# A transformer step on one core: 52 squared down tiles, and the first seven up tiles taken in two token halves

## The reference, cut to what matters

```python
def peer_ffn(h, w_query, sub_keys1, sub_keys2, expert_down, expert_up):
    ...
    expert_idx = jnp.take_along_axis(cand_idx, pos, axis=-1)
    gates = jax.nn.softmax(top_v, axis=-1).astype(h.dtype)
    ...
        u = jnp.take(expert_down, idx_blk, axis=0)
        act = jax.nn.gelu(jnp.einsum('bpd,bphkd->bphk', h_blk, u))
        vv = jnp.take(expert_up, idx_blk, axis=0)
        return jnp.einsum('bphk,bphkd->bpd', g_blk * act, vv)
```

## Time and profile before

| what | us |
|---|---|
| three runs | 1527.0 (1525.01 to 1530.42) |
| profiled execution, its own time | 1524.74 |
| its span | 1523.1 |
| TensorE busy in it | 1483.8 (97%) |
| VectorE, ScalarE, GpSimd busy | 1100.7, 661.1, 426.1 |

### The profile page before, as it was taken

How to read it: one execution, slowest core, us unless ns; L and a number is a source line. 1 busy time by engine, 2 the same in 40 slices (tenths; PEclk the granted TensorE clock), 3 DMA queues, 4 the chain that set the end, 5 groups by cost and what they waited for, 6 DMA issues and landing times.

```text
span 1523.1 us, 25244 instructions
## 1 busy us (share of the span) xinstructions
PE 1483.8 (97%) x9787; PEld 1253.5 (82%) x9787; DVE 1100.7 (72%) x1942; ACT 661.1 (43%) x1013; POOL 426.1 (28%) x285
## 2 busy tenths in 40 slices
PE   8999999999999978999999999999999999999998
PEld 5777878875655577599999999999999888888887
DVE  5888788674675664767888887777776767777776
ACT  4556453643421511334443444444444445455453
POOL 0000000000000200018888888888883000000000
PEclk9999999999999999999999999999999999999999
DMA  9777573357555930456767667777775777777776
GB/s 340 280 247 247 198 261 129 138 206 230 186 207 194 367 133 17 142 167 154 160 146 140 139 145 162 167 161 160 158 162 123 239 237 240 240 241 240 238 239 229
DMA packets 183306, 297.24 MB, mean 195 GB/s; under 512 B 51818, under 2 KB 92546, under 8 KB 183188
## 3 DMA queue, kind: packets, MB, share of 16 engines
q1 hardware_dynamic: 136528, 277.08, 54.8%
q0 software_dynamic: 39296, 8.55, 8.3%
q10 hardware_dynamic: 7364, 9.99, 2.0%
HBM read 276.54 MB, written 19.03 MB: 194 GB/s over the span
## 4 chain that ended last, share of the span: by engine, by line
PE 58%; POOL 26%; issue 7%; DVE 5%; ACT 2%; DMA 1%; ACTq 1%; SPq 0%; DVEq 0%; POOLq 0%
POOL c_dram L2635 26%; PE bank L568 14%; PE bank L570 14%; PE bank L572 14%; PE bank L563 5%; ACTq L2087 1%; PE bank L540 1%; PE bank L918 1%; PE bank L930 1%; PE bank L620 1%; PE bank L929 1%; DVE gt L1291 1%; PE bank L1111 0%; PE bank L613 0%; PE bank L553 0%
## 5 line engine op out<-in xcount | busy, mean ns | idle before, releaser
L2635 POOL DMA_INDIRECT c_dram<-gates,places x256 | 403.6, 1577 | 149.0 <-issue 77.7
L568 PE MATMUL bank<-hT_high,dT_high 128*128 128x256 f32 x1024 | 294.9, 288 | 0.0
L570 PE MATMUL bank<-hT_low,dT_high 128*128 128x256 f32 x1024 | 288.5, 282 | 0.0
L572 PE MATMUL bank<-hT_high,dT_low 128*128 128x256 f32 x1024 | 288.3, 282 | 0.0
L1310 DVE TENSOR_TENSOR dT_low<-bank,dT_high 128x512 fp32r<-128x512 f32 x256 | 164.0, 681 | 91.3 <-ACT dT_high L2528 90.1
L2540 ACT CAST up_high<-slot 128x1024 fp32r<-128x1024 f32 x128 | 134.3, 1049 | 160.9 <-DMA slot<-in_expert_up_dram 160.9
L568 PE MATMUL bank<-up_high,A_high 128*128 128x512 f32 x512 | 199.9, 391 | 1.3 <-DVE A_low L1310 1.3
L570 PE MATMUL bank<-up_low,A_high 128*128 128x512 f32 x512 | 200.7, 392 | 0.0
L572 PE MATMUL bank<-up_high,A_low 128*128 128x512 f32 x512 | 199.2, 389 | 0.0
L568 PEld LDWEIGHTS bank<-hT_high,dT_high 128*128 128x128 f32 x1024 | 194.1, 190 | 0.2 <-issue 0.2
L572 PEld LDWEIGHTS bank<-hT_high,dT_low 128*128 128x128 f32 x1024 | 193.5, 189 | 0.0
(11 more groups left out here) (451 smaller groups left out, 2459.2 us busy)
## 6 DMA issues: line engine op xcount, KB each, us to landing
slot<-in_expert_up_dram SPq DMA_DIRECT2D x128, 512.0 KB, 3.5
slot<-in_expert_down_dram SPq DMA_DIRECT2D x89, 512.0 KB
slot<-in_w_in_dram SPq DMA_DIRECT2D x41, 1024.0 KB, 5.2
slot<-in_expert_down_dram SPq DMA_DIRECT2D x156, 128.0 KB
P<-in_w_ada_dram SPq DMA_DIRECT2D x16, 1024.0 KB, 7.7
c_dram<-zeros SPq DMA_DIRECT2D x1, 16384.0 KB, 50.9
slot<-c_dram SPq DMA_DIRECT2D x128, 128.0 KB, 3.5
slot<-in_w_in_dram SPq DMA_DIRECT2D x6, 2048.0 KB, 8.9
```

What stands on the lines that cost most here:

```text
L568: pe.matmul(o, lhsT=lhs_high.bitcast(F32R), rhs=rhs_high.bitcast(F32R), start=start, stop=False, skip_group_check=True)
L570: pe.matmul(o, lhsT=lhs_high.bitcast(F32R), rhs=rhs.bitcast(F32R), start=False, stop=False, skip_group_check=True)
L572: return pe.matmul(o, lhsT=lhs.bitcast(F32R), rhs=rhs_high.bitcast(F32R), start=False, stop=stop, skip_group_check=True)
L2635: g.indirect_dma_start(C_dram, bass.IndirectOffsetOnAxis(ap=places[:, x, k:k + 1], axis=0), gates[:, x, k:k + 1], None, compute_op=ALU.add ...
```

## The change

`SQUARED` takes two of three tiles above 49 instead of one of two: 52 instead of 39. The ring of up tiles has seven places (`RING`); the three new ones lie where the down tiles were, and are loaded when the last down tiles have been transposed. The up stage is now a list of 135 passes: tiles 0 to 6 for the first 128 tokens, the same tiles for the other 128 tokens, then tiles 7 to 127 whole. A pass of one token half has two banks, 6 matmuls, and operations of 128 columns where there were 256. All counts (`gated`, `weighed`, `tile_done`, the ring of gates) go by the pass number u. The gates of the first passes wait for the scatters of t = 0 alone, those of pass 7 for t = 1. In SyncE's queue the gates of pass p + 4 now stand behind up tile p, which waits until pass p is finished.

```diff
@@ -173,7 +173,8 @@
-    down_in, up_in = [sem(f"down{j}_in") for j in range(3)], [sem(f"up{j}_in") for j in range(4)]
+    RING = 7
+    down_in, up_in = [sem(f"down{j}_in") for j in range(3)], [sem(f"up{j}_in") for j in range(RING)]
...
-    up_tile = [slot[1][:, j * D:(j + 1) * D] for j in range(4)]
+    up_tile = [slot[1][:, j * D:(j + 1) * D] for j in range(4)] + [down_tile[j] for j in (2, 0, 1)]
+    up_low = [carve_at(f"up_low{j}", slot_at + 4 * at * D, D) for j, at in enumerate((4, 5, 6, 7, 2, 0, 1)[0:RING])]
...
+    up_hi_free = [N_KEYS - 3, N_KEYS - 3, N_KEYS - 2, N_KEYS - 2, N_KEYS - 1, N_KEYS - 1, N_KEYS - 1]
+    up_tile_free = {4: N_KEYS - 3, 5: N_KEYS - 2, 6: N_KEYS - 1}
+    FIRST, SECOND, BOTH = range(1), range(1, TT), range(TT)
+    passes = ([(p, FIRST) for p in range(RING)] + [(p, SECOND) for p in range(RING)] +
+              [(p, BOTH) for p in range(RING, N_KEYS)])
+    pass_of = {p: u for u, (p, ts) in enumerate(passes)}
+
+    def up_tokens(u):
+        ts = passes[u][1]
+        return slice(ts.start * P, ts.stop * P)
...
-    SQUARED = [n for n in range(N_KEYS) if n > 49 and n % 2 == 1]
+    SQUARED = [n for n in range(N_KEYS) if n > 49 and n % 3 != 0]
...
+    def pe_tile_up(u):
+        p, ts = passes[u]
+        pe.wait_ge(weighed, u + 1)
         pe.wait_ge(up_split, p + 1)
-        for b in range(4):
-            m = pe_up_part(p, b)
+        for b in range(2 * ts.start, 2 * ts.stop):
+            m = pe_up_part(u, b)
         m.then_inc(tile_done, 1)
...
+    def v_gate(u):
+        p, tok = passes[u][0], up_tokens(u)
         clear(v, ("down", p))
-        v.wait_ge(coeff_in[p % 4], 16 * (p // 4 + 1))
-        v.tensor_tensor(G[:, p, :], G[:, p, :], coeff[p % 4], ALU.mult).then_inc(gated, 1)
+        v.wait_ge(coeff_in[u % 4], 16 * (u // 4 + 1))
+        v.tensor_tensor(G[:, p, tok], G[:, p, tok], coeff[u % 4][:, tok], ALU.mult).then_inc(gated, 1)
...
     def v_experts():
         v_gate(0)
         v_gate(1)
-        v_split_up(0)
-        v_weigh(0)
-        for p in range(N_KEYS):
-            if p + 2 < N_KEYS:
-                v_gate(p + 2)
-            if p + 1 < N_KEYS:
-                v_split_up(p + 1)
-                v_weigh(p + 1)
+        for u, (p, ts) in enumerate(passes):
+            if ts != SECOND:
+                v_split_up(p)
+            v_weigh(u)
+            if u == RING - 1:
+                v_gate(RING)
+                v_gate(RING + 1)
+            elif u != RING - 2 and u + 2 < len(passes):
+                v_gate(u + 2)
...
     def a_split_up(p):
-        a.wait_ge(up_in[p % 4], 16 * (p // 4 + 1))
-        if p > 3:
-            a.wait_ge(tile_done, p - 3)
+        a.wait_ge(up_in[p % RING], 16 * (p // RING + 1))
+        if p < RING:
+            held(a, ("down", up_hi_free[p]))
         else:
-            held(a, ("down", N_KEYS - 3 + p // 2))
-        a.copy(up_hi[p % 4].bitcast(F32R), up_tile[p % 4]).then_inc(up_high, 1)
-
-    def a_weigh(p):
-        a.wait_ge(gated, p + 1)
-        if p > 3:
-            a.wait_ge(tile_done, p - 3)
-        a.copy(A_high[p % 4].bitcast(F32R), G[:, p, :]).then_inc(a_high_made, 1)
+            a.wait_ge(tile_done, pass_of[p - RING] + 1)
+        a.copy(up_hi[p % RING].bitcast(F32R), up_tile[p % RING]).then_inc(up_high, 1)
+
+    def a_weigh(u):
+        p, tok = passes[u][0], up_tokens(u)
+        a.wait_ge(gated, u + 1)
+        if u > 3:
+            a.wait_ge(tile_done, u - 3)
+        a.copy(A_high[u % 4][:, tok].bitcast(F32R), G[:, p, tok]).then_inc(a_high_made, 1)
...
+            if n == N_KEYS - 2:
+                for p in (0, 1):
+                    a_split_up(p)
+                    a_weigh(p)
             if n == N_KEYS - 1:
-                a_split_up(0)
-                a_weigh(0)
+                a_split_up(2)
+                a_split_up(3)
+                a_weigh(2)
             a_tile_gelu(n)
             if n == 1:
                 a_gates(0, range(1, 2), range(1, 2))
             if n in (15, 30, 45):
                 a_gates(n // 15)
-        for p in range(1, N_KEYS):
-            a_weigh(p)
-            a_split_up(p)
+        for u in range(3, RING):
+            a_weigh(u)
+            if u + 1 < RING:
+                a_split_up(u + 1)
+        for u in range(RING, len(passes)):
+            a_weigh(u)
+            if u >= RING + 4 and passes[u - 4][0] + RING < N_KEYS:
+                a_split_up(passes[u - 4][0] + RING)
...
     def s_up(p):
-        if p > 3:
-            sp.wait_ge(tile_done, p - 3)
-        sp.dma_start(up_tile[p % 4], I["expert_up_2"][0][p * P:(p + 1) * P, :]).then_inc(up_in[p % 4], 16)
-
-    def s_coeff(p):
-        if p > 3:
-            sp.wait_ge(gated, p - 3)
-        sp.dma_start(coeff[p % 4], C_dram[p * P * S:(p + 1) * P * S].rearrange("(e n) o -> e (n o)", n=S)
-                     ).then_inc(coeff_in[p % 4], 16)
+        if p >= RING:
+            sp.wait_ge(tile_done, pass_of[p - RING] + 1)
+        elif p in up_tile_free:
+            held(sp, ("turn", up_tile_free[p], 1))
+        sp.dma_start(up_tile[p % RING], I["expert_up_2"][0][p * P:(p + 1) * P, :]).then_inc(up_in[p % RING], 16)
+
+    def s_coeff(u):
+        p, ts = passes[u]
+        if u in (0, RING):
+            for h in range(2):
+                sp.wait_ge(scattered[ts.start][h], 16 * TOPK * PEER_H // 2)
+        if u > 3:
+            sp.wait_ge(gated, u - 3)
+        sp.dma_start(coeff[u % 4][:, up_tokens(u)],
+                     C_dram[p * P * S:(p + 1) * P * S].rearrange("(e n) o -> e (n o)", n=S)[:, up_tokens(u)]
+                     ).then_inc(coeff_in[u % 4], 16)
 
...
         for n in range(3, N_KEYS):
             s_down(n)
-        for t in range(TT):
-            sp.wait_ge(scattered[t][1], 16 * TOPK * PEER_H // 2)
-        for p in range(4):
-            s_coeff(p)
-        for p in range(4, N_KEYS):
-            s_coeff(p)
+        for u in range(4):
+            s_coeff(u)
+        for u in range(4, RING):
+            s_up(u)
+            s_coeff(u)
+        for u in range(RING, RING + 4):
+            s_coeff(u)
+        for p in range(RING, N_KEYS):
             s_up(p)
+            if pass_of[p] + 4 - RING < len(passes):
+                s_coeff(pass_of[p] + 4 - RING)
+        for u in range(len(passes) + 4 - RING, len(passes)):
+            s_coeff(u)
```

More of the change, by code:

```diff
@@ L454, in program @@
     coeff = [slot[0][:, 3 * D + j * S:3 * D + (j + 1) * S] for j in range(4)]
-    up_tile = [slot[1][:, j * D:(j + 1) * D] for j in range(4)]
-    cursor[0] = slot_at + 4 * KT * CW
-    up_low = [carve(f"up_low{j}", D) for j in range(4)]
+    up_tile = [slot[1][:, j * D:(j + 1) * D] for j in range(4)] + [down_tile[j] for j in (2, 0, 1)]
+    up_low = [carve_at(f"up_low{j}", slot_at + 4 * at * D, D) for j, at in enumerate((4, 5, 6, 7, 2, 0, 1)[0:RING])]
     cursor[0] = hT_at
@@ L460, in program @@
     cursor[0] = lasting_top
-    dT_low, dT_high, up_hi = [], [], [None] * 4
+    dT_low, dT_high, up_hi = [], [], []
     for j in range(3):
@@ L472, in program @@
     A_low = [carve(f"A_low{n}", S) for n in range(N_KEYS)]
-    for j, at in enumerate((4 * 4 * D, 5 * 4 * D, 0, 4 * D)):
-        cursor[0] = lasting_top + at
-        up_hi[j] = carve(f"up_high{j}", D)
+    for j, at in enumerate([lasting_top + 4 * x * D for x in (4, 5, 0, 1, 2, 3)][0:min(RING, 6)] + [hT_at][0:RING - 6]):
+        up_hi.append(carve_at(f"up_high{j}", at, D))
+    up_hi_free = [N_KEYS - 3, N_KEYS - 3, N_KEYS - 2, N_KEYS - 2, N_KEYS - 1, N_KEYS - 1, N_KEYS - 1]
[7 more added lines that the diff above has]
+        return slice(ts.start * P, ts.stop * P)
     cursor[0] = persistent_top + 4 * TT * w_in2.shape[1]
@@ L1194, in pe_tile_down, with pe_up_part @@
         m.then_inc(filled(("down", n)), 1)
[L1196 to L1202, removed]
+    def pe_up_part(u, b):
+        p, t, at = passes[u][0], b // 2, slice(b % 2 * CW, (b % 2 + 1) * CW)
+        return pe_three(bank[b], A_low[p][:, t * P:(t + 1) * P], A_high[u % 4][:, t * P:(t + 1) * P],
+                        up_low[p % RING][:, at], up_hi[p % RING][:, at], p == 0, u == len(passes) - 1)
+    def pe_tile_up(u):
+        p, ts = passes[u]
+        pe.wait_ge(weighed, u + 1)
         pe.wait_ge(up_split, p + 1)
-        for b in range(4):
-            m = pe_up_part(p, b)
+        for b in range(2 * ts.start, 2 * ts.stop):
+            m = pe_up_part(u, b)
         m.then_inc(tile_done, 1)
     def pe_last_tiles():
-        pe.wait_ge(weighed, N_KEYS)
+        pe.wait_ge(weighed, len(passes))
         pe.wait_ge(up_split, N_KEYS)
         for b in range(4):
-            pe_up_part(N_KEYS - 2, b)
-            pe_up_part(N_KEYS - 1, b).then_inc(bank_summed, 1)
+            pe_up_part(len(passes) - 2, b)
+            pe_up_part(len(passes) - 1, b).then_inc(bank_summed, 1)
     def pe_experts():
@@ L1223, in pe_experts @@
             fill(("acc", b), b)
-        for p in range(N_KEYS - 2):
-            pe_tile_up(p)
+        for u in range(len(passes) - 2):
```

(51 more changed lines are left out.)

## The result

The changed kernel takes 1559.94 us (1553.06 to 1566.07, four runs), the kernel before 1528.63 us (1525.01 to 1530.42, four runs beside it). The ratio is 1.0207, with a 95% interval of 1.0156 to 1.0258: slower by 31 us. 1555 was forecast, with 1530 to 1571 as the range.

What follows compares the result with a forecast made beforehand. Two chains were taken to end together, TensorE's down products and GpSimd's scatters, with TensorE bounding the up stage. A gain of 11.1 us, then losses of 6.0 and 35, made +30 on 1524.7: 1555 us, range 1530 to 1571.

Steps and rivals of the forecast that it cites:

- The down stage: Down products: thirteen turns fewer save 11.8 us, ending at 1154.3 instead of 1166.07, with VectorE keeping up.
- C: Down stage does not become faster, since VectorE or the squared loads set its pace: 1565 us; chance 0.07.
- D: Added transposes slow GpSimd's scatters by up to 29 us, and pass 7 with them: up to 1584 us; chance 0.02.
- The halves: Start of the up stage: seven passes of 6 matmuls take 9.6 us, from 1154.3 to 1163.9.
- Pass 7: After the first-half passes: TensorE starts it at 1165.1 instead of 1166.61, leaving the up stage 11.1 us ahead.
- which GpSimd ends no earlier: Before pass 7: it still waits for the scatters of t = 1, the last issued at 1158.70 in the kernel before.
- Passes 7 to 13: Early up stage: gates of pass 11 stand behind up tile 7; pass 14 starts at 1180.7, 6.0 us lost.
- The order in SyncE's queue: Up stage, passes 14 to 130: gates' cover 0.80 us too little; 3.05 us a tile instead of 2.747, 35 us lost.
- the handover from `A_low` to TensorE: Up stage, last link from up tile issue to pass: 0.67 us of a chain of 6.09 us.
- The sum: Whole kernel: -11.1 + 6.0 + 35 = +30 us on the profiled execution's 1524.7 us, giving 1555.
- Rival B: Up stage: gates come in time, TensorE stays the bound, only the gain is left: 1514 us; chance 0.11.
- The estimate of 3.5: Up stage: DMA fit for 640 KB of up tile and gates, 3.5 us in place of 3.95; sum would be 1533.

Runs made afterwards that it cites:

- The swap there and back: Changed kernel with gates ahead of the up tile: 1526.98 us, ratio 0.9983; kernel before with gates behind it: 1561.18 us, ratio 1.0199.
- Three halves with the wait filled: Changed kernel with gates ahead of up tiles, three halved tiles instead of seven, 36 unused matmuls in the wait: 1521.5 us, ratio 0.9961 against the kernel before.
- the kernel without halves: Changed kernel with gates ahead of up tiles and all tiles whole (52 squared tiles, ring of seven): 1529.42 us, ratio 1.0002 against the kernel before.
- the probe: 14 VectorE products, both operands in SBUF, added to the kernel without halves just before the first gate product, beside the last scatters: 1529.52 us, one execution.
- the probe with one operand in PSUM: The same 14 VectorE products added to the kernel without halves, with one operand in PSUM instead of SBUF: 1528.84 us, one execution.

## Why the prediction was right, and where it was off

- **The down stage.** Forecast to end at 1154.3. It ended at 1157.97, or 1154.2 without the 3.8 us of the earlier stages. VectorE kept up, as the window from 1000 to 1100 shows, and rivals C and D (as it was put, by the transposes) fall.
- **The halves.** The seven first-half passes ran from 1157.80 to 1167.60, when the last matmul ends, without a wait: 9.8 us, with 9.6 forecast.
- **Pass 7.** Forecast for 1165.1, started at 1173.72, or 1169.9 without the 3.8. The step that failed is "which GpSimd ends no earlier": it ended later, by 5.3 us (0.4 us of it came back between the last scatter and pass 7). The prediction weighed VectorE's added transposes against the scatters, and not the gate products and low parts that the halves move beside them.
- **Passes 7 to 13.** 15.6 us were forecast from pass 7 to pass 14 and 17.5 measured (1173.72 to 1191.20). The clock of 0.51 after the wait, 10 matmuls at 0.43 instead of 0.23 us, comes to 2.0 us, which the sum didn't have; the other terms nearly cancel.
- **The order in SyncE's queue.** Forecast 3.05 us a tile, measured 3.04; in the old kernel with the same order 3.03. The swap there and back shows the cause. Of the terms, the handover from `A_low` to TensorE was 0.47 instead of 0.67 us (median of the passes that waited), and some gates came later than 3.95, so two small errors met.
- **The sum.** Against the execution profiled before, 30 us were forecast; the medians differ by 31.3. That they lie so near is in part luck. In the profiled execution, without the 3.8 us of the earlier stages, the loss was 34.5 us: 4.8 for pass 7 and 1.9 for passes 7 to 13 on top of the forecast, less 2.2 from pass 14 to the end, where 372.4 us were forecast and 370.2 measured. The other three executions took 1553 to 1566 us; what lay late in them no trace shows.
- **Rival B** had its threshold at a gate product 3.15 us behind the up tile. In the changed kernel the 112 gate products that waited behind up tiles 14 to 127 came 3.53 to 5.53 us behind it, 3.85 at the median. The estimate of 3.5 from the Trainium skill ("DMA: Bandwidth & Descriptors", section "Anatomy of one DMA — SWDGE (gpsimd) path") is below the least of them. The sum by that estimate comes to 1532 or 1536, without or with the 0.10 us for the first tile after a wait, and not to 1533.

## What to carry to other kernels

When a queue serves in order, count for each transfer how many units of the bound engine's work lie between what its issue waits for and its use, also for the small transfer queued behind a large one: here one unit fewer cost 0.3 us a turn, on average, in 117 turns. Work moved into a wait pays only if the wait's end does not move, the stage after it can be fed at the new pace, and the engine does not idle into a lower clock; of 9.6 us moved here 2.4 remained. Three halves with the wait filled, 4.1 us moved, took 0.4% off the kernel without halves by the ratios.

## What the runs showed of the hardware

- TensorE's granted clock fell to its lower level (0.50 and 0.51 in the windows, 1.2 GHz) behind waits of 14.48, 6.12, 3.64 and 2.58 us, for some 3 to 5 us each time; matmuls of 512 columns then came every 0.43 us instead of 0.23. With the wait filled by matmuls, and behind the wait of 1.31 us, it stayed at 1.00.
- VectorE operations with both operands in SBUF can hold up GpSimd's indirect DMAs: in the probe two of them took 1.73 and 2.10 us instead of 1.55, and beside the mixed operations of the changed kernel one took 5.85. Beside the probe with one operand in PSUM they stayed at 1.55 or 1.56, and beside the added transposes (from 910 us on) at 1.55 to 1.57. The Trainium skill ("SBUF — State Buffer", section "SBUF: two separate sides") says that a VectorE operation in a 2-port mode, or one with two SBUF inputs against a GpSimd operation that reads SBUF, contends with GpSimd for one shared port pair. The two probes agree with that in direction, if the indirect DMA counts as such a reader; the size of the hold isn't explained. The transposes have one SBUF input, so the two-input part of that rule gives rival D no mechanism.
- The gate product came 3.95 us behind the up tile's issue at the median in the kernel before, and 3.85 us in the changed one, where the DMA engines' share was 0.67 instead of 0.74: the pair of transfers became hardly shorter when the stage slowed down.
